# Gate and up biases of 32 experts as products of 64 rows each, issued as neighbours

## What is computed

```python
g = xb @ w_gate[e] + b_gate[e]
u = xb @ w_up[e] + b_up[e]
g = jnp.minimum(g, SWIGLU_LIMIT)
u = jnp.clip(u, -SWIGLU_LIMIT, SWIGLU_LIMIT)
h = (u + 1) * (g * jax.nn.sigmoid(SWIGLU_ALPHA * g))
return h @ w_down[e] + b_down[e]
```

## Time and profile before

| | us |
|---|---|
| median of 3 runs (1545.01 to 1546.97) | 1545.95 |
| the profiled execution | 1545.41 |
| its span, from the first to the last instruction | 1543.7 |
| PE busy in the span | 1451.5 (94%) |
| DVE busy | 1271.7 (82%) |
| ACT busy | 1054.1 (68%) |
| POOL busy | 180.3 (12%) |

### The profile page before, as it was taken

One profiled execution on the slowest core, in us unless ns is written; L12 is line 12 of the kernel. 1 busy time (PEld: TensorE's weight loads), 2 busy tenths in 40 slices (PEclk: granted clock), 3 DMA queues, 4 the chain that ended last, 5 costly groups with the idle time before them and its releaser, 6 DMA issues.

```text
span 1543.7 us, 21413 instructions
## 1 busy us (share of the span) xinstructions
PE 1451.5 (94%) x7157; PEld 1064.4 (69%) x7157; DVE 1271.7 (82%) x1234; ACT 1054.1 (68%) x959; POOL 180.3 (12%) x186
## 2 busy tenths in 40 slices
PE   6999996875999999999999999999999999999993
PEld 5999865743677777777777777777777777777772
DVE  4344466355999999999999999999999999999995
ACT  4445433343777878787878777787778787777775
POOL 3000131034000000000011000000000011000000
PEclk9999997765999999999999999999999999999997
DMA  7311322137999999999999999999999999999994
GB/s 225 117 55 55 98 74 90 46 109 279 316 374 364 379 371 375 374 375 375 373 373 368 367 366 381 367 381 375 376 372 374 373 370 374 361 374 370 385 360 151
DMA packets 170596, 464.78 MB, mean 301 GB/s; under 512 B 14228, under 2 KB 28192, under 8 KB 170288
## 3 DMA queue, kind: packets, MB, share of 16 engines
q1 hardware_dynamic: 157528, 432.03, 75.4%
q0 software_dynamic: 8880, 24.00, 6.6%
q10 hardware_dynamic: 4152, 8.31, 1.6%
HBM read 447.90 MB, written 23.59 MB: 305 GB/s over the span
## 4 chain that ended last, share of the span: by engine, by line
PE 85%; issue 8%; DVE 2%; ACT 2%; POOL 1%; DVEq 1%; ACTq 1%; DMA 0%; POOLq 0%; SPq 0%
PE ps L1725 81%; PE ps L1728 4%; DMA acc_rows<-reg_a,pass_tok 0%; POOL slot_rows L677 0%; DVE ring_r L451 0%; ACT ring L1121 0%; DVE ring L1144 0%; DVE ring_r L1164 0%; DVE ring L1716 0%; POOL reg_z L643 0%; DVE reg_b L1323 0%; POOL acc_rows L709 0%; DVEq L1691 0%; DVEq L1325 0%; ACT ring L765 0%
## 5 line engine op out<-in xcount | busy, mean ns | idle before, releaser
L1725 PE MATMUL ps<-ring_r,reg_z_r 128*96 128x512 f32 x4608 | 1099.6, 395 | 2.5 <-DVE ring_r L451 2.5
L1725 PEld LDWEIGHTS ps<-ring_r,reg_z_r 128*96 128x96 f32 x4608 | 738.5, 162 | 311.8 <-DVE ring_r L451 3.0
L1056 ACT ACTIVATE ring_r<-ring 128x2048 fp32r<-128x2048 f32 x387 | 735.9, 1915 | 168.9 <-PE ps L1725 166.1
L451 DVE TENSOR_TENSOR ring_r<-ring,ring_r 128x2048 fp32r<-128x2048 f32 x355 | 797.6, 2283 | 58.0 <-ACT ring_r L1056 58.0
L728 POOL DMA_INDIRECT acc_rows<-reg_a,pass_tok x32 | 49.0, 1530 | 1016.4 <-ACT reg_a L1073 884.2
L1725 PE MATMUL ps<-reg_a_r,ring_r 128*128 128x264 f32 (+1 forms) x576 | 110.1, 286 | 0.0
L1725 PE MATMUL ps<-ring_r 128*128 128x256 f32 (+3 forms) x372 | 104.0, 329 | 4.3 <-DVE ring_r L1495 4.3
L1725 PEld LDWEIGHTS ps<-reg_a_r,ring_r 128*128 128x128 f32 x576 | 90.6, 188 | 2.4 <-issue 2.2
L1079 ACT ACTIVATE reg_z_r<-ps 128x384 fp32r<-128x384 f32 x130 | 58.9, 479 | 44.7 <-PE ps L1728 35.5
L1654 DVE TENSOR_TENSOR ring_r<-ring,ring_r 128x1024 fp32r<-128x1024 f32 x64 | 77.6, 1213 | 0.0
L1725 PEld LDWEIGHTS ps<-ring_r 128*128 128x128 f32 (+1 forms) x372 | 68.1, 185 | 13.3 <-DVE ring_r L1495 4.4
(11 more groups left out here) (320 smaller groups left out, 966.7 us busy)
## 6 DMA issues: line engine op xcount, KB each, us to landing
ring<-in_w_gate SPq DMA_DIRECT2D x131, 1024.0 KB, 7.2
ring<-in_w_up SPq DMA_DIRECT2D x128, 1024.0 KB, 5.7
ring<-in_w_down SPq DMA_DIRECT2D x128, 1024.0 KB, 8.4
ring<-in_w_in SPq DMA_DIRECT2D x9, 1024.0 KB, 6.4
ring<-in_w_out SPq DMA_DIRECT2D x4, 1024.0 KB, 5.2
ring<-in_x_prompt SPq DMA_DIRECT2D x4, 512.0 KB, 8.7
reg_a<-in_x_prompt SPq DMA_DIRECT2D x4, 512.0 KB, 6.1
xhat_rows<-reg_w ACTq DMA_DIRECT2D x4, 512.0 KB, 2.9
```

What stands on the lines that cost most here:

```text
L451: return eng.tensor_tensor(rest_r(k), w, rounded_r(k).bitcast(F32), ALU.subtract)
L1056: act.activation(rounded_r(k), ring[:, slot_of(k), :], ACT.Copy).then_inc(hi_ready, 1)
L1725: return pe.matmul(out, lhsT, rhs, start=start, stop=stop, skip_group_check=True)
```

## The change

Gate and up biases now share 128 rows: rows 0 to 63 are gate (rounded, rest), rows 64 to 127 are up. There are no zero rows, so POOL's two memsets and the semaphore `pads_made` are gone. `id128` has ones for four groups of 32 rows (eight selections on POOL in place of three). The bias of an expert is four products of 64 rows: `pick[0:64]` by rows 0 to 63 into banks 0 and 1, `pick[64:128]` by rows 64 to 127 into banks 2 and 3, alternating, all at the head of the expert. In the routing stage the four loads stand together where the two for gate stood, ACT's rounding is three copies (one of them over all rows) where it was six, and DVE's two subtractions wait for one semaphore value.

```diff
-            for base, cols_ in ((0, slice(0, NE)), (-NE, slice(0, NE + 1)), (0, slice(NE, NE + 1))):
-                v = id128[0:64, cols_]
-                pool.affine_select(v, v, [[-1, v.shape[1]]], ALU.not_equal, 1.0, base=base, channel_multiplier=1)
+            for base in range(0, P, NE):
+                for v in (id128[:, 0:NE], id128[:, NE:NE + 1]):
+                    pool.affine_select(v, v, [[-1, v.shape[1]]], ALU.not_equal, 1.0, base=-base, channel_multiplier=1)
                 pool.drain()
...
             pool.memset(slot_tab, 0.0)
             pool.drain()
-            for m in range(2):
-                pool.memset(e_bias[m][64:P, :], 0.0)
-            pool.drain()
-            pool.engine_nop().then_inc(pads_made, 1)
...
-            def load_bias(m):
-                for half in range(2):
-                    act.dma_start(e_bias[m][32 * half:32 * half + 32, :], a[("b_gate", "b_up")[m]][0]
-                                  ).then_inc(bias_rows_in, 16)
+            def load_bias():
+                for n in range(4):
+                    act.dma_start(gu_bias[32 * n:32 * n + 32, :], a[("b_gate", "b_up")[n // 2]][0]).then_inc(bias_rows_in, 16)
...
+            def round_bias():
+                act.wait_ge(bias_rows_in, 16 * 4)
+                act.activation(gu_tmp_r, gu_bias, ACT.Copy)
+                act.drain()
+                for n in (0, 64):
+                    last = act.activation(gu_bias_r[n:n + 32, :], gu_bias[n:n + 32, :], ACT.Copy)
+                last.then_inc(bias_hi, 1)
...
-            def bias_rows_of(m, bank, u):
+            def bias_rows_of(u):
 
                 for q in range(2):
-                    mm(ps[bank + q][0:CAP, :], pick[:, u, :], e_bias_r[m][:, 512 * q:512 * q + 512], stop=False)
+                    for m in range(2):
+                        rs = slice(64 * m, 64 * m + 64)
+                        mm(ps[2 * m + q][0:CAP, :], pick[rs, u, :], gu_bias_r[rs, 512 * q:512 * q + 512], stop=False)
...
-                            bias_rows_of(0, 0, u)
+                            bias_rows_of(u)
                             for n in range(4):
                                 product(k + n, 0, eX, p12)
-                            bias_rows_of(1, 2, u)
                             for n in range(4, 7):
                                 product(k + n, 2, eX, p12)
```

More of the change, by code:

```diff
@@ L211, in hybrid_step @@
         id128 = reg_t[:, 3990:3990 + NE + 1]
[L213 to L217, removed]
+        gu_bias, gu_bias_r = reg_t[:, 2960:3984], split_view("reg_t", 4120, 2960, [P, D])[:, :]
+        gu_tmp_r = split_view("reg_c", 2304, D, [P, D])[:, :]
+        down_b, down_b_r = reg_b[0:96, 0:D], split_view("reg_b", 2048, 0, [96, D])[:, :]
+        down_tmp_r = split_view("reg_z", NZ * TT, z0 + 3 * D, [64, D])[32:64, :]
         pick = split_view("reg_p", 1536, 1280, [P, 2 * CAP])[:, :].rearrange("p (b n) -> p b n", b=2)
@@ L338, in hybrid_step @@
         ident_made, masks_made, rows_made, iotas_made = sem("ident_made"), sem("masks_made"), sem("rows_made"), sem("iotas_made")
-        pads_made = sem("pads_made")
         eps_made, rms_ready = sem("eps_made"), sem("rms_ready")
@@ L965, in gate_exps, with round_down_bias @@
                                accum_out=rs1[0:r, 1:2]).then_inc(gexp_ready, 1)
-            def load_bias(m):
-                for half in range(2):
-                    act.dma_start(e_bias[m][32 * half:32 * half + 32, :], a[("b_gate", "b_up")[m]][0]
-                                  ).then_inc(bias_rows_in, 16)
+            def load_bias():
+                for n in range(4):
+                    act.dma_start(gu_bias[32 * n:32 * n + 32, :], a[("b_gate", "b_up")[n // 2]][0]).then_inc(bias_rows_in, 16)
             def load_down_bias():
                 for third in range(3):
[L974 to L987, removed]
+                    act.dma_start(down_b[32 * third:32 * third + 32, :], a["b_down"][0]).then_inc(down_in, 16)
+            def round_down_bias():
+                act.wait_ge(down_in, 48)
+                act.activation(down_tmp_r, down_b[32:64, :], ACT.Copy)
+                act.activation(down_b_r[64:96, :], down_b[64:96, :], ACT.Copy)
+                act.activation(down_b_r[0:32, :], down_b[0:32, :], ACT.Copy).then_inc(bias_hi, 1)
+            def round_bias():
[5 more added lines that the diff above has]
+                last.then_inc(bias_hi, 1)
             act.wait_ge(*dstate_ready)
@@ L1001, in _ @@
             act.dma_start(sc_mix[0].rearrange("b (h n) -> (b h) n", h=MH), h32).then_inc(mixs_out, 16)
-            load_bias(0)
+            load_bias()
             load_down_bias()
@@ L1032, in _ @@
             act.activation(oT, ps[3][:, 256:320], ACT.Copy).then_inc(sample_act, 1)
-            round_bias(2)
+            round_down_bias()
             act.wait_ge(*datt_ready)
@@ L1040, in _ @@
             gate_exps(3)
-            load_bias(1)
             store_xhat(3)
-            round_bias(0)
-            round_bias(1)
+            round_bias()
             act.wait_ge(g3_psum, 1)
@@ L1496, in mix_of_attention, with rest_of_down_bias, rest_of_bias @@
                                   ALU.subtract).then_inc(mixs_ready, 1)
[L1498 to L1501, removed]
+            def rest_of_down_bias():
+                dve.wait_ge(bias_hi, 1)
+                dve.tensor_tensor(down_b_r[32:64, :], down_b[32:64, :], down_tmp_r.bitcast(F32), ALU.subtract).then_inc(bias_lo, 1)
+            def rest_of_bias():
+                dve.wait_ge(bias_hi, 2)
+                for n in (32, 96):
+                    last = dve.tensor_tensor(gu_bias_r[n:n + 32, :], gu_bias[n:n + 32, :], gu_tmp_r[n:n + 32, :].bitcast(F32),
+                                             ALU.subtract)
+                last.then_inc(bias_lo, 1)
             def add_down_bias(i):
@@ L1606, in _ @@
             places(1)
-            rest_of_bias(2)
+            rest_of_down_bias()
             gates_of(2)
@@ L1615, in _ @@
             scale_rows(3)
-            for m in range(2):
-                rest_of_bias(m)
+            rest_of_bias()
             places(3)
@@ L2024, in down_bias @@
                     mm(ps[2 + q][0:rows(i), :], gT_r[:, i * P:i * P + rows(i)],
-                       e_bias_r[2][:, 512 * q:512 * q + 512]).then_inc(ybias_psum, 1)
+                       down_b_r[:, 512 * q:512 * q + 512]).then_inc(ybias_psum, 1)
             def keys_T(half):
```

## The result

The changed kernel takes 1579.05 us (median of 4 runs, 1578.78 to 1581.03), the kernel before 1545.67 (4 runs beside them): a ratio of 1.0218, 95% interval 1.02 to 1.0235. It is slower by 33 us. The range forecast ended at 1546.5.

What follows compares the result with a forecast made beforehand. PE sets the end in the experts, so PE's savings count as long as DVE keeps up. From 1545.41 us, 3.6 saved in the experts and 0.7 in the routing stage gave 1541.1 us; range 1538.5 to 1546.5.

Steps and rivals of the forecast that it cites:

- POOL's eight selections in place of three: POOL, ahead of the experts: selections end near 238 us, DVE first needs them at 269.90, so no cost.
- Experts, 3.6 us saved: Experts on PE: 464 ns saved by overlapping pairs less 350 ns added, 114 ns an expert over 32.
- a lag of 0 and of 85 ns: Experts: a pair's second weights load with the first's (3.6 us saved) or only behind them (0.9 us).
- (a): Experts: second product's weights wait for the first's, lag 85 ns, only 0.9 us saved there; 1543.8 us, chance 0.32.
- (b): Experts: the 64-row products run one after the other, 9.3 to 11.2 us lost; about 1555 us, chance 0.14.
- (c): Experts: no change of rows takes place and pairs still overlap, 14.8 us saved; 1529.9 us, chance 0.06.
- The two changes of rows: Experts on PE: going from 128 rows to 64 and back costs 90 + 85 = 175 ns each, 350 ns an expert.
- the third 0.23 us behind the first: Sign at each expert's head: the third of four bias products starts 0.23 us after the first.
- Routing stage, 0.7 us saved: Stage before the experts: fewer copies let `places(3)` start 0.7 us sooner, released by PE's ranks at 339.5.
- slip: Routing stage: two DMA starts moved ahead of ACT's copy of keys delay the stage by 0.93 us (0.7 to 1.25).
- the 1.7 us that stood as an end: Routing stage: the best end of the 0.7 us term, 1.7 us saved if there is no slip.
- The cover of DVE: Experts: DVE keeps up though it has 464 ns less, costed at nothing; if cover is gone, 2 us lost.

Runs made afterwards that it cites:

- e1: The kernel before with seven idle instructions added to POOL's program ahead of its loop over passes: 1580.47 us, ratio 1.0222.
- e2: The changed kernel with one more idle instruction in POOL's program ahead of its loop over passes: 1544.02 us, ratio 0.9984.
- e9: The changed kernel with one of POOL's two drains in a row behind the selections taken out: 1543.79 us, ratio 0.9981.
- e8: e3 without the two up bias products, leaving up bias out of the output: 1543.45 us, ratio 0.9985.
- e5: e3 with the up bias's two DMA starts put back behind the last experts' gates, as in the kernel before: 1541.21 us, ratio 0.9971.
- e3: The changed kernel with id128 made by five selections instead of eight, so POOL's loop stands where it stood before: 1544.16 us, ratio 0.9985.
- e7: e3 with the four bias products reordered, both of gate and then both of up: 1544.41 us, ratio 0.9994.

## Why the prediction was wrong

- **The step that failed**: "POOL's eight selections in place of three [...] end near 238 us, [...] so they cost nothing". As work they do cost nothing. As code they moved the loop over passes by seven instructions, to the one place of the four tried where skipped passes take 9 us each; that is 35 us, more than all terms of the sum together (e1, e2, e9). None of the rivals had a mechanism behind the experts, and none asked what POOL does when the work is done.
- **Experts, 3.6 us saved**: right in kind, 2.7 measured (85 ns an expert for 114). No row of the kernel before decided between a lag of 0 and of 85 ns, and 0 was right: the first two of the four last 0.468 us each and lie within 0.47, their four loads of weights together take 0.24 us, and two products have the time of one (e8), so rivals (a) and (b) fall; the 0.33 us ahead of the first product of 64 rows is there, so (c) falls too. That 85 ns of loading are added at a change of rows was my estimate, from a product behind a transposition; no row quoted shows it. In the traces the loads of the 64-row products start at 913.56, with their product at 913.57 and behind 0.39 us without a load, where the load of the bias in the kernel before starts at 912.62 for a product at 912.85. The two changes of rows cost about what was forecast. From the last product of 128 rows to the next are 0.96 us (913.24 to 914.20), of which 0.23 is a normal step, and the product behind lasts 0.47 in place of 0.40: 0.81 in all for 0.93 before, 0.12 by these rows, near the 0.114. Only the sign "the third 0.23 us behind the first" was wrong, and against the forecast's own price: the first pair's products last 0.468 where the second pair's last 0.393, and the second pair starts 0.31 behind the first, 0.08 more than a normal step. The remaining 0.03 between 0.12 and 0.085 isn't placed.
- **Routing stage, 0.7 us saved**: wrong in sign, 1.4 lost in the profile. The gain from fewer copies, with `places(3)` released by PE, was right: e5, which has no slip, gains the 1.7 us that stood as an end. The slip was mis-sized: 0.93 forecast, 1.2 at the copy of keys, and 3.1 at `places(3)`, since I took a stage that starts later to be as long as before, and it has a lower clock for longer (0.68 from 320 to 326 us where e5 has 0.96).
- **The cover of DVE** held: PE waits 0.0 us.

With the loop at a good place the change alone comes to 1544.16 (e3), inside the range; without the two starts ahead of the copy to 1541.21 (e5), where the forecast was 1541.1. That this one agrees is luck: the kernel is not the one forecast, and the terms differ, 2.7 and 1.7 for 3.6 and 0.7.

## What to carry to other kernels

An edit to an engine that is nearly always idle can still cost time, if its program has a loop (POOL is busy 11% here, and the edit cost 35 us): look at what each engine does at the very end, and at jumps over long bodies. If a small edit makes a kernel slower by something that no engine works on, put one idle instruction ahead of the loop and measure again, which gave 35 us back in e2. A DMA's start on an engine that others wait for is paid there, 0.46 us each here, and more than once if the work behind it then meets a lower clock: a slip of 1.2 us became 3.1.

## What was not expected of the hardware

- One instruction's shift of a loop's head changes a skipped pass from 0.65 us to 8.6 (changed kernel, its last four head instructions: (1571.6 - 1545.8) / 3).
- Four products of 64 rows and 512 columns, two on each half of the rows, take 0.71 us where the two of one half take 0.70 (e8), and they take 0.71 in either order of the program (changed kernel, e7).
- Where the rows change from 128 to 64 and back, a step of 0.23 us becomes 0.33, and the first product behind it lasts 0.47 us where the others last 0.39.
